# Second mixer of a two-layer trunk: two key parts moved ahead of a tile, substitution steps spread differently, an inverse tile moved to another place

## The reference, cut to what matters

```
def odd_mixer(h, w_in, w_out, ...):
    p = h @ w_in
    z, xbc, dt_raw, rw = split_cols(p, (SSM_INNER, SSM_CONV_W, SSM_HEADS, RW_IN))
    xbc = jax.nn.silu(causal_conv(xbc, ssm_conv_w, ssm_conv_b))
    xs, Bm, Cm = split_cols(xbc, (SSM_INNER, SSM_BC, SSM_BC))
    ...
    y = ssd_chunked(xh, dt, A, Bm.reshape(...), Cm.reshape(...))
    y = y.reshape(bsz, T, SSM_INNER) * jax.nn.silu(z.astype(F32))
    y_ssm = group_rmsnorm(y, ssm_norm, SSM_GROUPS).astype(h.dtype)
    rw = rw + (token_shift(rw) - rw) * rw_mu
    r, k, v, wd, ad, gd = split_cols(rw, (RW_W, RW_W, RW_W, RW_DECAY_LORA, RW_AAA_LORA, RW_GATE_LORA))
    ...
    kk = kk / jnp.maximum(jnp.sqrt(jnp.sum(kk * kk, axis=-1, keepdims=True)), 1e-12)
    ...
    yr = rwkv7_scan(rh, decay.reshape(hd), kh, vh, kk, kk * ah)
    ...
    return jnp.concatenate([y_ssm, y_rw], axis=-1) @ w_out

def rwkv7_scan(r, w, k, v, kk, kka):
    def step(S, inp):
        r_t, w_t, k_t, v_t, kk_t, b_t = inp
        sa = jnp.einsum('bhvk,bhk->bhv', S, kk_t)
        S = S * w_t[:, :, None, :] - sa[..., None] * b_t[:, :, None, :] + v_t[..., None] * k_t[:, :, None, :]
        return S, jnp.einsum('bhvk,bhk->bhv', S, r_t)
```

## Time and profile before

| | |
|---|---|
| median of 3 runs | 1358.56 us (1357.12 to 1362.73) |
| profiled execution, own time | 1360.57 us |
| its span, first to last instruction | 1358.4 us |
| busy PE, POOL, DVE, ACT | 96%, 49%, 42%, 40% of the span |
| mean granted clock of PE | 0.981 |

### The profile page before, as it was taken

How to read it: one execution, slowest core, us unless ns; L and a number is a source line. 1 busy time by engine, 2 the same in 40 slices (tenths; PEclk the granted TensorE clock), 3 DMA queues, 4 the chain that set the end, 5 groups by cost and what they waited for, 6 DMA issues and landing times.

```text
span 1358.4 us, 18265 instructions
## 1 busy us (share of the span) xinstructions
PE 1300.2 (96%) x6685; PEld 1041.8 (77%) x6685; DVE 568.1 (42%) x913; ACT 536.7 (40%) x880; POOL 659.7 (49%) x810
## 2 busy tenths in 40 slices
PE   5999978999999999999989899899999999999997
PEld 3877756788888888887767677788878888888886
DVE  4438665421221211244689955477531121121233
ACT  5335664341331322435662524753442232231332
POOL 4653224565554555565344534212555555554553
PEclk9999988999999999999989899899999999999999
DMA  9322101333333333333212221000333333333331
GB/s 276 82 77 76 48 16 47 94 93 93 93 93 93 93 93 93 94 92 93 62 48 76 79 62 47 1 2 1 93 93 94 93 93 93 93 93 93 94 91 62
DMA packets 198036, 108.87 MB, mean 80 GB/s; under 512 B 4570, under 2 KB 195280, under 8 KB 197968
## 3 DMA queue, kind: packets, MB, share of 16 engines
q1 hardware_dynamic: 197552, 107.88, 27.8%
q0 software_dynamic: 416, 0.07, 0.0%
HBM read 105.83 MB, written 2.10 MB: 79 GB/s over the span
## 4 chain that ended last, share of the span: by engine, by line
PE 83%; DVE 9%; ACT 4%; issue 2%; DMA 0%; POOL 0%; DVEq 0%; SPq 0%; ACTq 0%
PE ps L904 23%; PE ps L905 23%; PE ps L906 23%; PE ps L891 2%; DVE arena L2346 1%; PE ps L945 1%; PE ps L1305 1%; PE ps L946 1%; PE ps L947 1%; DVE arena L2464 1%; DVE y_mix L2467 1%; DVE relu L2330 1%; PE ps L1062 1%; PE ps L1093 1%; PE ps L1379 1%
## 5 line engine op out<-in xcount | busy, mean ns | idle before, releaser
L810 POOL TENSOR_TENSOR w_lo<-raw_w,w_hi 128x256 fp32r<-128x256 f32 x760 | 617.9, 844 | 589.6 <-ACT w_hi L1458 589.6
L1458 ACT ACTIVATE w_hi<-raw_w 128x1024 fp32r<-128x1024 f32 x190 | 201.1, 1058 | 533.1 <-PE ps L906 422.8
L904 PE MATMUL ps<-hn_hi,w_hi 128*128 128x512 f32 x880 | 357.4, 406 | 2.7 <-POOL w_lo L810 1.8
L906 PE MATMUL ps<-hn_hi,w_lo 128*128 128x512 f32 x880 | 349.4, 397 | 0.0
L905 PE MATMUL ps<-hn_lo,w_hi 128*128 128x512 f32 x880 | 349.2, 397 | 0.0
L904 PE MATMUL ps<-hid_hi,w_hi 128*128 128x512 f32 x576 | 227.6, 395 | 0.0
L906 PE MATMUL ps<-hid_hi,w_lo 128*128 128x512 f32 x576 | 227.5, 395 | 0.0
L905 PE MATMUL ps<-hid_lo,w_hi 128*128 128x512 f32 x576 | 227.5, 395 | 0.0
L904 PEld LDWEIGHTS ps<-hn_hi,w_hi 128*128 128x128 f32 x880 | 166.4, 189 | 49.8 <-issue 8.3
L905 PEld LDWEIGHTS ps<-hn_lo,w_hi 128*128 128x128 f32 x880 | 166.5, 189 | 41.7 <-issue 2.9
L906 PEld LDWEIGHTS ps<-hn_hi,w_lo 128*128 128x128 f32 x880 | 166.0, 189 | 40.7
(11 more groups left out here) (392 smaller groups left out, 1277.0 us busy)
## 6 DMA issues: line engine op xcount, KB each, us to landing
raw_w<-in_w_up SPq DMA_DIRECT2D x64, 512.0 KB, 4.0
raw_w<-in_w_down SPq DMA_DIRECT2D x64, 512.0 KB, 4.0
raw_w<-in_o_w_in SPq DMA_DIRECT2D x27, 512.0 KB, 3.8
raw_w<-in_e_w_in SPq DMA_DIRECT2D x19, 512.0 KB, 3.8
raw_w<-in_e_w_out SPq DMA_DIRECT2D x8, 512.0 KB, 3.4
raw_w<-in_o_w_out SPq DMA_DIRECT2D x8, 512.0 KB, 3.5
rwkv_raw<-in_x SPq DMA_DIRECT2D x4, 512.0 KB, 8.6
out<-arena SPq DMA_DIRECT2D x8, 256.0 KB, 2.9
```

The costliest lines, as they stand in the source:

```text
L810: nc.gpsimd.tensor_tensor(w_lo[:, n % CUT, ks], raw_w[:, n % RING, ks], w_hi[:, n % CUT, ks].bitcast(F32), ALU.subtract).then_inc(w_cut, 1)
L904: mm(o, a_hi, b_hi, start=(k == 0), stop=False)
L906: ins = mm(o, a_lo, b_hi, start=False, stop=(k == KT - 1))
L1458: A(w_hi[:, n % CUT], raw_w[:, n % RING], ACT.Copy).then_inc(w_high, 1)
```

## The change

Four edits, all in the second mixer. First, DVE does `key_part(0)` and `key_part(1)` ahead of `shift(6)`. Second, between the convolved tiles 12 to 16 DVE does two substitution steps a tile and no longer three; the five steps left over are done behind the last of these tiles, around `ssd_front(0)` and `ssd_weights(0)`. Third, the tile `inv_t[0]` moves from `late` to the place of `sub_inv` in `y_mix`, which is dead once `inv_ready` is set; so its memset and `fill_columns(0)` can be done in slot 24, not behind the front. `inv_d` is stored as 64 columns a head in place of 128, beside `inv_p`, and one memset zeroes both; `t1` and `square_out` move to `late`. Fourth, PE does `p_low` and `mats` 1 ahead of the four `z_tok`, and ACT does `fill_rows(0)` ahead of draining `rv_tok`.

```diff
@@ rwkv_chunks
     for n in range(NT):
         yield "rv_tok", n
+    yield "p_low", 0
+    yield from products(0, 1)
     for n in range(NT):
         yield "z_tok", n
-    yield "p_low", 0
-    yield from products(0, 1)
     yield from low_merge(0)
@@ tiles
-        inv_d, inv_t0, inv_p = (cut(late, (4 + j) * 1024, 8, P) for j in range(3))
-        inv_t = (inv_t0, cut(stage_t, 0, 8, P))
+        inv_t = (cut(y_t, 3072, 8, P), cut(stage_t, 0, 8, P))
+        inv_dp = cut(late, 4096, 1024)
+        inv_d, inv_p = (cut(late, 4096 + j * 512, 8, HALF) for j in range(2))
         inv_q = cut(late, 7168, 8, HALF)
-        inv_p = cut(late, 6 * 1024, 8, HALF)
...
-        square_out = cut(y_t, 3584, 256)
+        square_out = cut(late, 5632, 256)
...
-        t1 = cut(y_t, 3072, 512)
+        t1 = cut(late, 5120, 512)
@@ POOL
+                    if n == base["in", 1] + 24:
+                        pool.wait_ge(S["inv_ready"], 1)
+                        nc.gpsimd.memset(inv_t[0], 0.0).then_inc(S["inv_zero"], 1)
                     if n == base["out", 1] + CUT - 1:
                         full(pool, "rw", 11)
-                        nc.gpsimd.memset(inv_t[0], 0.0).then_inc(S["inv_zero"], 1)
-                        nc.gpsimd.memset(inv_d, 0.0).then_inc(S["inv_zero"], 1)
-                        nc.gpsimd.memset(inv_p, 0.0).then_inc(S["inv_zero"], 1)
+                        nc.gpsimd.memset(inv_dp, 0.0).then_inc(S["inv_zero"], 1)
@@ ACT
+            def fill_columns(n):
+                if n >= 2:
+                    full(act, "u", n - 2)
+                act.wait_ge(S["inv_ready"], 1)
+                act.wait_ge(S["inv_zero"], (1, 3, 4, 5)[n])
+                for q in range(P // SUB):
+                    rows = slice(q * SUB, (q + 1) * SUB)
+                    ins = A(inv_t[n % 2][rows, :, rows], inv_cols[rows, :, n * 8:n * 8 + 8].rearrange("p c j -> p j c"),
+                            ACT.Copy)
+                ins.then_inc(S["inv_filled"], 1)
+
+            def fill_rows(n):
+                if n:
+                    full(act, "t_high", n - 1, 1)
+                act.wait_ge(S["inv_zero"], 2)
+                for q in range(P // SUB):
+                    rows, own = slice(q * SUB, (q + 1) * SUB), slice(q % 2 * SUB, (q % 2 + 1) * SUB)
+                    ins = A(inv_d[rows, :, own], inv_rows[rows, :, n * 8:n * 8 + 8].rearrange("p c j -> p j c"), ACT.Copy)
+                ins.then_inc(S["inv_filled"], 1)
...
+                if j == 24:
+                    fill_columns(0)
...
-            fill_columns(0)
+            fill_rows(0)
             for t in range(NT):
                 full(act, "rv_tok", t)
             for t in range(NT):
                 drain(v_tok[:, t, :], "rv_tok", t)
-            fill_rows(0)
@@ DVE
             take_staged(6)
-            shift(6)
             key_part(0)
             key_part(1)
+            shift(6)
             take_staged(7)
...
             for i in range(12, 17):
                 take_staged(i)
-                substitute(3 * i - 28, 3 * i - 27)
+                substitute(2 * i - 16, 2 * i - 15)
                 conv_staged(i)
-                substitute(3 * i - 27, 3 * i - 25)
+                substitute(2 * i - 15, 2 * i - 14)
...
-            substitute(23, 25)
+            substitute(18, 20)
             ssd_front(0)
-            substitute(25, 26)
+            substitute(20, 22)
             ssd_weights(0)
-            substitute(26, 31)
+            substitute(22, 31)
```

More of the change, by code:

```diff
@@ L1324, in odd @@
                             ins = mm(o[0:HALF, hh * HALF:(hh + 1) * HALF], inv_p[0:HALF, hh, :],
-                                     inv_d[0:HALF, hh, 0:HALF], start=True, stop=True)
+                                     inv_d[0:HALF, hh, :], start=True, stop=True)
                         close(ins, *item)
@@ L1331, in odd @@
                                 r = slice(pair * HALF, (pair + 1) * HALF)
-                                ins = mm(o[r, hh * HALF:(hh + 1) * HALF], inv_d[r, hh, r], inv_p[r, hh, :],
+                                ins = mm(o[r, hh * HALF:(hh + 1) * HALF], inv_d[r, hh, :], inv_p[r, hh, :],
                                          start=True, stop=True, skip_group_check=True)
@@ L1350, in odd @@
                             hh = 4 * half + j
-                            ins = mm(o[0:HALF, j * HALF:(j + 1) * HALF], inv_d[0:HALF, hh, 0:HALF],
+                            ins = mm(o[0:HALF, j * HALF:(j + 1) * HALF], inv_d[0:HALF, hh, :],
                                      inv_q[0:HALF, hh, :], start=True, stop=True)
@@ L1848, in turned @@
                 drain(bb_tok[:, n % 2, :], "rb_tok", n)
[L1850 to L1859, removed]
-                if n >= 2:
-                    full(act, "u", n - 2)
-                fill_blocks(n, inv_cols, inv_t[n % 2], (1, 4, 5, 6)[n])
-            def fill_rows(n):
-                if n:
-                    full(act, "t_high", n - 1, 1)
-                fill_blocks(n, inv_rows, inv_d, 2)
             def high_merge(n):
@@ L2597, in keep_pairs @@
                 if n == 0:
-                    dve.wait_ge(S["inv_zero"], 3)
+                    dve.wait_ge(S["inv_zero"], 2)
                 o = heads8(full(dve, "p_low", n))
```

## The result

| | before | changed |
|---|---|---|
| median, same chip | 1360.64 us (1357.12 to 1363.01, 4 runs) | 1343.86 us (1341.88 to 1345.63, 4 runs) |
| ratio, 95% interval | | 0.9887, 0.9864 to 0.991 |
| profiled execution: span, own time | 1358.4, 1360.57 us | 1343.6, 1345.63 us |

The change makes the kernel about 15 us (1.1%) faster: the profiled executions differ by 14.9 us in their own time and 14.8 us in span, where 12.7 were forecast. The medians differ by more, 16.8 us, since the kernel before measured 1360.64 us beside the changed one and not the 1358.56 that the forecast started from. 1343.86 lies in the range of 1341.0 to 1350.8 and 2.0 us under the forecast of 1345.9.

The account below looks back on a forecast made before the run. PE, busy 96% of the span, bounds the kernel, and DVE's late line sets its waits in the front. 9.1 (5.5 + 3.6) + 0.7 + 2.9 = 12.7 us off the profiled execution; from the median 1358.56, 1345.9 us, range 1341.0 to 1350.8.

Parts of the forecast that it names:

- rivals with a lower clock in the front: Slots 15 to 20: several short waits drop PE's clock to 1.2 GHz; 1361.2 us at three slots; chance 0.02.
- with no gain at all: Front: moved waits win nothing, PE's first wait returns at slots 14 to 17; about 1356.5 us; chance 0.05.
- as forecast: Whole kernel: the likeliest case, a gain of 10.5 to 14.5 us, 1344 to 1348 us; chance 0.64.
- contention rival: DVE in the front: removed work was what POOL slowed; gain 15.6 us, so 1343.0 us; chance 0.14.
- Key parts: DVE ahead of `shift(6)`: moving two key parts into its idle stretch gains 5.5 us.
- 3.6 us: DVE ahead of `take_staged(16)`: four deferred steps gain 3.6 us, their undisturbed price, with POOL slowing the neighbours instead.
- the removed work was the contended work: DVE in the front: gains 7.6 and up to 7.6 us, capped by PE's 14.5; 1343.0 us; chance 0.14.
- Clock behind `ssd_front` 0: PE behind the front's last waits: a better held clock gains 0.7 us, between 0 and 2.2.
- Behind the front: Fill and order edits: shorter waits at `p_low`, `d` and `t_low` gain 2.9 us, bounds 1.4 to 4.0.
- With one fill gone from here that silu is 2.65 us earlier: ACT behind the front: moving the first fill to slot 24 starts the silu of z 2.65 us earlier.
- z's turns fill what was waiting time: PE behind the front: with `p_low` waiting only for DVE's mask, z's turns run in former waiting time.
- Nothing gives it back: Behind the mixer: PE is the bound and starts earlier as a whole, so the summed 12.7 us stay.

Follow-up runs that it names:

- e1: Kernel before with only `key_part(0)` and `key_part(1)` moved ahead of `shift(6)`: 1353.85 us, ratio 0.9969.
- e2: Kernel before with only the substitution steps cut to two a tile in place of three: 1350.49 us, ratio 0.9926.
- g4: Changed kernel with one substitution step a tile, between `take_staged` and `conv_staged`: 1339.18 us, ratio 0.9848.
- e4: Changed kernel with PE's old order, `z_tok` ahead of `p_low` and `mats` 1: 1342.36 us, ratio 0.9875; run again 1340.59 us, 0.9881.
- g1: Changed kernel with PE's old order (`z_tok` first) and one substitution step a tile, behind `conv_staged`: 1340.82 us, ratio 0.9877.
- f2: Changed kernel with DVE's first mask ahead of its last `ssd_back`: 1340.52 us, ratio 0.9885.
- h2: Changed kernel with `fill_columns(0)` behind the front again, ahead of `fill_rows(0)`, memset kept in slot 24: 1344.94 us, ratio 0.9887.
- h1: Changed kernel with one substitution step a tile ahead of `conv_staged` and DVE's first mask ahead of its last `ssd_back`: 1335.88 us, ratio 0.983.
- e3: Changed kernel with the key-part move and the step reduction undone, so third and fourth edits alone: 1358.84 us, ratio 0.9999 to the kernel before.

## Why the prediction was right, and where it was not

**Right.** The mechanism of the main part: DVE's line bounds the front, PE follows it, and two edits shorten it without eating each other (e1, e2, table). The key parts take 5.38 us in the idle stretch (5.3 forecast), the wait at `sub` 0 is gone, and with it 2.2 us of clock. DVE's smaller number decides over PE's larger one (e1, 6.7 cut to 6.1). Nothing waits for the deferred steps, and ACT's cut behind the moved fill still waits 1.28 us before it starts. The rivals with a lower clock in the front, or with no gain at all, did not come.

**How much of the hit is luck.** The total came out closer than its terms. In the profiled executions DVE's line gave 1.9 us more than forecast and the clock behind `ssd_front` 0 1.8 more; 2.0 us were given back at the end, where the forecast said that nothing would be. 14.8 us lie just outside the 10.5 to 14.5 that the prediction allowed for "as forecast", and nearer to the 15.6 of the contention rival than to 12.7.

**Sizes.**
- Key parts: 5.5 forecast, 6.0 measured (5.3 to 7.6 given). At `take_staged(7)` all 7.6 us are there (691.37 - 674.0 against 683.41 - 673.68 behind `kk_inv`); 1.6 of them are lost again by `take_staged(10)`, as other work of DVE comes to stand there.
- Steps: the term "3.6 us" measured 4.9 (3.6 to 7.6 given). I had put the four steps at their undisturbed price and let POOL's contention fall on the neighbours whole. It did not. In the trace of before, the last step behind the taps of each of the tiles 12 to 15, which is the work that goes, takes 1.28, 1.32, 0.92 and 1.31 us, 4.8 in all; the four tiles got shorter by 1.28, 1.32, 0.91 and 1.40 us. The second of them, with the next `take_staged`:

```profile
749.21 0.83 DVE L2464 TENSOR_TENSOR arena<-y_mix 128x252 f32<-128x252 f32 x1
750.08 0.42 DVE L2467 TENSOR_TENSOR y_mix<-y_mix,arena 128x252 f32<-128x252 f32 x1
...
750.64 0.68 DVE L2330 TENSOR_TENSOR relu<-ps,rms 128x512 f32<-128x512 f32 x1
```

  Three of the eight operations overlap POOL's subtractions and take 0.81 to 0.83 us, the other five 0.40 to 0.43. So here the contention went with the steps that met it. In g4 it did not go whole: the four steps taken away there had cost 6.4 us and freed 4.6. The port rule of the Trainium skill, page "SBUF — State Buffer", section "Who interferes with whom", was weighed in the prediction: read for all removed steps it would have given 7.6. The trace agrees with the rule itself, for the three operations. The rival "the removed work was the contended work" is right in this part, by 1.3 us.
- Together DVE's 10.9, not 9.1. The waits of PE left at `x_tok`, `ssd_front` 0 and for POOL are 1.5 + 0.8 + 1.3 = 3.6 us, not 5.4.
- Clock behind `ssd_front` 0: 0.7 forecast with 2.2 as the most, 2.5 measured. `ssd_front` 0 to `ssd_back` 0 took 13.5 us in all ten executions that have fewer steps between the tiles (the changed kernel twice, e2, e4 twice, g1, f2, h2, g4, h1: 13.46 to 13.48), and 16.0, 15.0 and 17.5 in before, e1 and e3, which don't. The granted clock of this stretch is 1.00 in the changed kernel and e2, and 0.82, 0.89 and 0.75 in before, e1 and e3. So the edit of the steps brings this; it is the one with which the waits for the silus are down to 2.3 us or less, from 6.0 and 4.5. "Near nothing, since a wait of one to two microseconds is still there" was the wrong guess.

**Wrong step.** Behind the front the size came out (3.0 from `mats` 0 to `p_high`, forecast 2.9), but not as forecast. "With one fill gone from here that silu is 2.65 us earlier" did not happen: behind `mats` 0 the silu starts after 11.8 us, before after 12.0. With PE's old order (e4) it is 2.7 us earlier, so the fill's time does leave the chain, but the fourth edit took that away. The fill's place in slot 24 isn't what frees it either: h2 moves the fill back and loses nothing. By the rows it is the memset's early place, since ACT had waited for it. "z's turns fill what was waiting time" is wrong too: e4 shows that the new order costs 1.1 us at `p_high`, and f2 that z's turns run slower behind `p_low`'s remaining wait because the clock drops. That wait for DVE's mask, 1.63 us, is what the forecast had put at nothing: it named the mask's end and priced no wait for it. The gain showed up as waits that went at `p_low`, `d` and `t_low` (1.4 + 1.8 + 0.8 us), less this new one. Its size hangs on the clock too: from `mats` 0 to `p_high` before and e1 took 17.4 us, e2 with the same order 18.4, the changed kernel 14.4. In the median, this third and fourth edit alone brought nothing that can be told from no change (e3, 0.9982 to 1.0015); 2.9 us would have been 0.9979.

**Given back.** "Nothing gives it back" is wrong as well, or at least not borne out. From `p_high` to `s_rw` 0 the changed kernel took 2.0 us more than before: 0.4 up to `u` 0, which now waits 1.6 us for DVE's mask, and 1.6 from `u` 0 to `s_rw` 0. I took this for chance when I ran the changed kernel again, but the runs don't say so. All five executions with PE's new order and DVE's mask late (the changed kernel twice, e3, h2, g4) take 11.1 us from `u` 0 to `s_rw` 0. Both with the early mask (f2, h1) take 8.0. Before and e1 take 9.5, e2 8.0. Against the edit as the only cause speaks e4, which took 9.5 us in one execution and 11.1 in the other. Whether the edit brings this loss stays open.

**Open.** The early memset without the new order on PE was not run on the kernel before, nor was the old order with DVE's mask early. Why the steps that g4 takes away bring only 2.8 us on PE is clear (no waits are left there). Whether PE's tile products could be placed otherwise was not tried.

## What to carry to other kernels

When an engine is saturated, look at the idle stretch just before it for work that is ready, and count what the next engine gains by the slower of the two, not by its own vanished wait. Between a hand-over to another engine and the use of its answer one small piece of work is free. Work behind the use of the answer is not: take that away and leave the first (g1 against g4). Work that is taken out of a contended stretch frees more than its undisturbed price: the four steps here cost 3.6 us undisturbed and 4.8 by their rows, and freed 4.9; those of g4 cost 3.6 and 6.4, and freed 4.6. When an engine waits for a memory to be zeroed, it is the zeroing that has to move, not the work behind it.

## What the runs showed of the hardware that was not expected

The same instructions take different times, in steps of some 1.6 us, by the granted clock, and in e4 they did so from one execution to the next. Windows from `ssd_back` 1 to 2, of before, of e4's second execution and of g4 (columns as above):

```profile
807.00:825.90 18.90, 18.90 (x97) 15.42 (x98) 9.62 (x13) 4.23 (x11) 6.18 (x7) 0.91 0.09 28
```

```profile
789.50:806.70 17.20, 17.18 (x96) 14.29 (x97) 9.68 (x13) 6.84 (x15) 6.25 (x7) 1.00 0.10 31
...
845.50:856.60 11.10, 11.05 (x144) 10.41 (x144) 2.12 (x4) 6.95 (x19) 7.20 (x7) 0.69 0.01 1
```

```profile
790.00:810.50 20.50, 20.49 (x96) 17.10 (x97) 9.66 (x13) 6.86 (x15) 6.22 (x7) 0.83 0.08 26
```

It is 17.2 us at clock 1.00, 18.9 at 0.91, 20.5 at 0.83, PE being busy all the time in each. Ahead of each stands the same wait of 2.0 us, at `ssd_back` 1. e4 itself took 18.9 in one execution and 17.2 in the other. From `u` 0 to `s_rw` 0 it was 8.0 us (f2, h1, e2; clock 1.00), 9.5 (before, e1, g1, e4; 0.82) or 11.1 (changed kernel twice, e3, h2, g4, e4 again; 0.69), with e4 on both sides once more. The Trainium skill, page "TensorE: Matmul & The Clock Gate", Part 1, says that the number of matmuls at the low clock at a kernel's start differs between runs of one kernel. e4's two executions agree, and show it in the middle of a kernel, behind waits of one to two microseconds. The two executions of the changed kernel show nothing of it. For reading: a difference of 1.6 to 3 us in one stretch of one profile is not the edit's until a second execution has it too; 13.29 twice against 14.35 and 14.36 is.

That a wait of 1.63 us ahead of small matmuls comes with a clock of 0.76 to 0.78 behind it was seen in this place in both executions of the changed kernel, in h2 and in g4; that one of 0.89 us comes with 1.00, in f2 and h1. No run changes the length of this wait alone, so that it is the cause is not shown.
